# Two tiles of x loaded and normalized earlier, output-stage loads reordered, last output unit split: a hybrid decoder layer on eight cores

## The reference

```
h    = rmsnorm(x, norm_pre)                       # x (4, 4096, 2048)
proj = h @ w_in                                   # columns: xa ga u v gb q gc, 1024 each
ya = pool_mixer(xa) * silu(ga)                    # windows 2, 4, 8, 16, then 256x256 maps
yb = u * (tril(w_s) @ layernorm(v) + b) * silu(gb)   # chunks of 128 positions, 8 heads
yc = softmax(q k^T / 16) v_m * silu(gc)           # k, v_m = rmsnorm(mem) @ w_kv, 4 heads
y  = concat(rmsnorm(ya), rmsnorm(yb), rmsnorm(yc))   # 3072 columns
x  = x + rmsnorm(y @ w_out, norm_post)
```

## Time and profile before

| | us |
|---|---|
| median of three runs | 1258.14 |
| the profiled execution | 1258.87 |
| span of its slowest core (core 3) | 1257.2 |
| spans of cores 0, 1, 2 | 1256.9, 1253.4, 1251.3 |
| spans of cores 4, 5, 6, 7 | 1255.0, 1255.8, 1254.6, 1256.1 |
| PE busy on core 3 | 1220.3 (97%) |
| DVE, ACT, POOL busy | 488.0, 475.9, 216.0 |

### The profile page before, as it was taken

How to read it: one execution, slowest core, us unless ns; L and a number is a source line. 1 busy time by engine, 2 the same in 40 slices (tenths; PEclk the granted TensorE clock), 3 DMA queues, 4 the chain that set the end, 5 groups by cost and what they waited for, 6 DMA issues and landing times.

```text
span 1257.2 us, 17843 instructions; the slowest of 8 cores (1251.3 to 1257.2 us)
## 1 busy us (share of the span) xinstructions
PE 1220.3 (97%) x6224; PEld 582.0 (46%) x6224; DVE 488.0 (39%) x782; ACT 475.9 (38%) x892; POOL 216.0 (17%) x205
## 2 busy tenths in 40 slices
PE   6889999999999999999999999999989999999997
PEld 3345544444444455555554444444434444444443
DVE  4167624332232233444443233333222454343434
ACT  4377733422222232222225555555632232223222
POOL 1000001221211011111121111111222222222222
PEclk9999999999999999999999999999999999999999
DMA  9945322554234452645435541441975492533231
GB/s 210 245 152 173 69 81 68 105 90 83 50 67 81 83 93 45 107 88 91 97 63 98 86 82 34 81 88 34 178 212 138 129 307 75 178 133 118 93 109 68
DMA packets 50938, 137.83 MB, mean 110 GB/s; under 512 B 22785, under 2 KB 35201, under 8 KB 37137
## 3 DMA queue, kind: packets, MB, share of 16 engines
q0 software_dynamic: 7632, 50.86, 24.3%
q1 hardware_dynamic: 43218, 85.83, 21.3%
HBM read 153.39 MB, written 29.36 MB: 145 GB/s over the span
## 4 chain that ended last, share of the span: by engine, by line
PE 90%; DMA 3%; DVE 2%; ACT 2%; issue 1%; SPq 0%; DVEq 0%; POOLq 0%; POOL 0%; ACTq 0%
PE ps L279 89%; DMA mem_pages<-x 2%; DMA mem_pages<-y_scr 2%; PE ps L282 1%; ACT mem_pages L391 1%; DVE mem_pages L395 1%; DVE mem_pages L1155 0%; ACT mem_pages L1030 0%; SPq L291 0%; ACT L1030 0%; DVE stat L1025 0%; DVE mem_pages L1127 0%; DVE mem_pages L1035 0%; DVE mem_pages L545 0%; ACT stat L256 0%
## 5 line engine op out<-in xcount | busy, mean ns | idle before, releaser
L279 PE MATMUL ps<-mem_pages 128*128 128x512 bf16 (+2 forms) x5760 | 1195.7, 369 | 7.9 <-DMA mem_pages<-y_scr 4.0
L279 PEld LDWEIGHTS ps<-mem_pages 128*128 128x128 bf16 x5760 | 555.7, 98 | 630.5 <-issue 22.8
L713 POOL TENSOR_TENSOR mem_pages<-mem_pages 128x512 f32<-128x512 f32 x72 | 91.1, 1266 | 599.9 <-ACT mem_pages L706 597.3
L700 ACT ACTIVATE mem_pages<-mem_pages,small_c 128x512 bf16<-128x512 f32 x96 | 68.8, 716 | 275.4 <-DVE mem_pages L772 148.1
L1127 DVE SCALAR_TENSOR_TENSOR mem_pages<-ps,stat,mem_pages 128x512 f32<-128x512 f32 x128 | 96.0, 750 | 166.8 <-PE ps L279 144.4
L1135 POOL TENSOR_TENSOR mem_pages<-mem_pages 128x512 f32<-128x512 f32 x64 | 81.1, 1267 | 257.3 <-ACT jk L1132 257.3
L1132 ACT ACTIVATE jk<-mem_pages 128x512 bf16<-128x512 f32 x64 | 40.3, 629 | 224.0 <-DVE mem_pages L1127 224.0
L903 DVE TENSOR_TENSOR mem_pages<-mem_pages 128x526 f32<-128x526 f32 (+3 forms) x80 | 56.1, 701 | 100.8 <-ACT mem_pages L897 95.8
L762 DVE TENSOR_TENSOR mem_pages<-ps,mem_pages 128x512 f32<-128x512 f32 x32 | 22.1, 691 | 141.3 <-PE ps L279 141.3
L732 ACT ACTIVATE mem_pages<-ps 128x512 f32<-128x512 f32 x96 | 54.5, 590 | 22.8 <-PE ps L279 19.4
L748 DVE CAST mem_pages<-ps 128x512 bf16<-128x512 f32 (+1 forms) x24 | 14.4, 601 | 124.6 <-PE ps L279 121.4
(11 more groups left out here) (66 smaller groups left out, 422.9 us busy)
## 6 DMA issues: line engine op xcount, KB each, us to landing
mem_pages<-w_pages POOLq DMA_DIRECT2D x44, 1024.0 KB, 12.9
mem_pages<-x SPq DMA_DIRECT2D x32, 1024.0 KB, 7.8
out<-mem_pages SPq DMA_DIRECT2D x15, 1024.0 KB, 4.7
y_scr<-mem_pages SPq DMA_DIRECT2D x96, 128.0 KB, 1.9
mem_pages<-y_scr SPq DMA_DIRECT2D x12, 1024.0 KB, 14.6
mem_pages<-w_pages POOLq DMA_DIRECT2D x8, 512.0 KB, 19.7
mem_pages<-mem SPq DMA_DIRECT2D x2, 1024.0 KB, 6.2
mem_pages<-mem_norm SPq DMA_DIRECT2D x1, 1024.0 KB
```

The source lines that it names most:

```text
L279: return lambda e: e.matmul(out, lhsT=lhsT, rhs=rhs, start=start, stop=stop)
L700: P.op("act", lambda e: e.activation(out=yv, in_=tmp, func=AF.Copy, scale=gbr[:, c:c + 1]), reads=[tmp_b[i], gbr_b], writes=[ring_b[r]])
L713: P.op("pool", lambda e: e.tensor_tensor(out=accl_v if last else acc, in0=acc, in1=dst, op=ALU.add), reads=[dst_b, acc_b[tb]], writes=[acc ...
```

## The change

Five edits:

- The load of tile 4 waits for the first half of v page (0,0) instead of page (0,1); that of tile 5 for the second half of page (1,0) instead of the first half of page (1,1). Loads 6 and 7 are as they were.
- `x_a(4)` stands ahead of the half layer norms of tiles 0 to 3; two of these follow it at once, the other two follow the first half of tile 4's transposes.
- The matmuls of tile 3's second column half are spread between those of tiles 0 to 2, so that tile 0's last group comes one group earlier; and for tile 4 the products with page (1,0) go ahead of tile 5's transposes.
- In `out_q` the third weight load goes last; the gain is asked for from block 10, the branch results from block 12.
- The last output unit (tile 15, last 512 columns) is two units of 256 columns, with a sum of squares each in new columns of `stat`; the four final pieces stay.

```diff
-    x_load(4, [W2[0].wtok])
-    x_load(5, [W4[0].wtok])
+    x_load(4, [W1[0].wtok])
+    x_load(5, [W3[1].wtok])
...
             v_mm(tt, 0, 1, part)
-            if part == 1:
-                v_ln_half(tt, 0)
     x_a(4)
+    for tt in range(2):
+        v_ln_half(tt, 0)
...
     x_pe(4, (7, 7), (0,))
+    for tt in range(2, 4):
+        v_ln_half(tt, 0)
     v_mm(0, 1, 1, 0)
     v_mm(1, 1, 1, 0)
     x_pe(4, (7, 7), (1,))
     v_mm(2, 1, 1, 0)
-    v_mm(3, 1, 0, 0)
-    v_mm(3, 1, 0, 1)
     for tt in range(3):
+        v_mm(3, 1, tt // 2, tt % 2)
         v_mm(tt, 1, 1, 1)
         v_ln_half(tt, 1)
         v_ln_end(tt)
         if tt == 1:
             x_a(5)
-    v_mm(3, 1, 1, 0)
     v_mm(3, 1, 1, 1)
...
+        if tt == 4:
+            v_mm(tt, 1, 0)
         if tt + 1 < NTT:
             x_pe(tt + 1)
...
-        v_mm(tt, 1, 0)
+        if tt > 4:
+            v_mm(tt, 1, 0)
         v_mm(tt, 1, 1)
...
-    out_q = [(3, 0, lambda: wo_load(0)), (3, 0, lambda: wo_load(1)), (3, 0, lambda: wo_load(2)),
-             (3, 13, lambda: y_load(0)), (2, 0, gp_load)]
+    out_q = [(3, 0, lambda: wo_load(0)), (3, 0, lambda: wo_load(1)), (1, 10, gp_load), (3, 12, lambda: y_load(0)),
+             (3, 13, lambda: wo_load(2))]
...
-        for db in range(4):
-            wo_unit(tt, db)
-        wo_final(tt, last=tt == NTT - 1)
+        last = tt == NTT - 1
+        for db in range(3 if last else 4):
+            wo_unit(tt, db, so=ST_SL + db if last else None)
+        if last:
+            wo_unit(tt, 3, 0, 256, ST_SL + 3)
+            wo_unit(tt, 3, 256, 256, ST_SL + 4)
+        wo_final(tt, last)
```

More of the change, by code:

```diff
@@ L249, in build_program @@
     ST_LH0, ST_LH1 = 352, 360
+    ST_SL = 368
     ST_EPS = 383
@@ L547, in v_ln_end @@
              reads=[bank[b], bank[b + 1], s1], writes=[vn_b[tt]])
-    W2, W3, W4 = wbuf(("v", 0, 1)), wbuf(("v", 1, 0)), wbuf(("v", 1, 1))
+    W1, W3, W4 = wbuf(("v", 0, 0)), wbuf(("v", 1, 0)), wbuf(("v", 1, 1))
     x_a(0)
@@ L1101, in take_orow @@
         p = dyn()
-        orow[tt] = (p, [nbuf("or%d_%d" % (tt, db), p) for db in range(4)], nbuf("orr%d" % tt, p))
+        orow[tt] = (p, [nbuf("or%d_%d" % (tt, db), p) for db in range(5)], nbuf("orr%d" % tt, p))
     def load_xres(tt):
@@ L1108, in load_xres, with wo_unit @@
         xres[tt] = (p, b)
-    def wo_unit(tt, db):
+    def wo_unit(tt, db, lo=0, n=512, so=None):
         tb = tt // 4
+        so = ST_SO + tt * 4 + db if so is None else so
         p, obs, _ = orow[tt]
-        ov = page_f(p)[:, db * 512:(db + 1) * 512]
+        ob = obs[db + (1 if lo else 0)]
+        c0 = db * 512 + lo
+        ov = page_f(p)[:, c0:c0 + n]
         bks = []
@@ L1118, in wo_unit @@
             Wo = w8(("wo", db, br))
-            fns = [mm(psb(b), yv[:, q, (tt % 4) * 128:(tt % 4 + 1) * 128], Wo[:, q, :], q == 0, q == 7)
+            fns = [mm(psb(b, 0, n), yv[:, q, (tt % 4) * 128:(tt % 4 + 1) * 128], Wo[:, q, lo:lo + n], q == 0, q == 7)
                    for q in range(8)]
@@ L1123, in wo_unit @@
         rc = ST_RBR + tt
-        P.op("act", lambda e: e.activation(out=ov, in_=psb(bks[0]), func=AF.Identity, scale=sc(rc)),
-             reads=[bank[bks[0]], rbr_b[tb]], writes=[obs[db]])
+        P.op("act", lambda e: e.activation(out=ov, in_=psb(bks[0], 0, n), func=AF.Identity, scale=sc(rc)),
+             reads=[bank[bks[0]], rbr_b[tb]], writes=[ob])
         for br in (1, 2):
             P.op("dve", lambda e, br=br: e.scalar_tensor_tensor(
-                out=ov, in0=psb(bks[br]), scalar=sc(rc + br * 16), in1=ov, op0=ALU.mult, op1=ALU.add),
-                reads=[bank[bks[br]], rbr_b[tb], obs[db]], writes=[obs[db]])
+                out=ov, in0=psb(bks[br], 0, n), scalar=sc(rc + br * 16), in1=ov, op0=ALU.mult, op1=ALU.add),
+                reads=[bank[bks[br]], rbr_b[tb], ob], writes=[ob])
         bfree(*bks)
[L1131 to L1134, removed]
+        P.op("act", lambda e: e.activation(out=jk_v[:, 0:n], in_=ov, func=AF.Square, scale=D ** -0.5,
+                                           accum_out=sc(so)),
+             reads=[ob], writes=[jk_b, so_b[tt]])
+        gv = page_f(gp["p"])[:, c0:c0 + n]
         P.op("pool", lambda e: e.tensor_tensor(out=ov, in0=ov, in1=gv, op=ALU.mult),
-             reads=[obs[db], gp["b"]], writes=[obs[db]])
+             reads=[ob, gp["b"]], writes=[ob])
     so_b = [Buf("so%d" % t) for t in range(NTT)]
@@ L1142, in wo_final @@
         stf = Buf("stf")
-        c0 = ST_SO + tt * 4
-        P.op("dve", lambda e: e.reduce_sum(out=sc(ST_FO + tt), in_=stat[:, c0:c0 + 4], axis=AX.X),
+        c0, cn = (ST_SL, 5) if last else (ST_SO + tt * 4, 4)
+        P.op("dve", lambda e: e.reduce_sum(out=sc(ST_FO + tt), in_=stat[:, c0:c0 + cn], axis=AX.X),
              reads=[so_b[tt]], writes=[stf])
@@ L1147, in wo_final @@
         xp, xb = xres[tt]
-        n = 4 if last else 1
-        w = 2048 // n
         rows = out_d[tt * 128:(tt + 1) * 128, :]
[L1151 to L1154, removed]
+        pieces = [(q, 1, obs[q:q + 1] if q < 3 else obs[3:]) for q in range(4)] if last else [(0, 4, obs)]
+        for q, n, ob in pieces:
+            o = page_f(p)[:, q * 512:(q + n) * 512]
+            xv = page_f(xp)[:, q * 512:(q + n) * 512]
             P.op("dve", lambda e, o=o, xv=xv: e.scalar_tensor_tensor(out=o, in0=o, scalar=sc(ST_FR + tt), in1=xv,
@@ L1157, in wo_final @@
                  reads=[stf, xb] + ob, writes=ob)
-            dma_sp(rows[:, q * w:(q + 1) * w], o, reads=ob, sem="d_o%d_%d" % (tt % 4, q))
+            dma_sp(rows[:, q * 512:(q + n) * 512], o, reads=ob, sem="d_o%d_%d" % (tt % 4, q))
         drop(p, xp)
```

## The result

The changed kernel took 1245.40 and 1246.18 us, the kernel before 1257.67 to 1259.98 (median 1258.62): a ratio of 0.9897 with a 95% interval of 0.9873 to 0.9921, about 13.0 us less (9.9 to 16.0), against 13.2 forecast.

A forecast was written before the change was run, and what follows sets the result against it. PE, busy 97% of the span, was taken as the bound, so gains lay only in its waits, slow stretches and tail. 7.0 + 5.6 + 0.6 = 13.2 us off gave 1244.9 us, range 1243.0 to 1248.0, chance 75%.

The forecast's parts named there:

- The start: First v products: tile 4's 4.49 wait and 1.67 slow stretch go, tile 0's last group comes 0.86 earlier; 7.0 us gained.
- The weights and tile 5: Loads at the start: earlier tiles delay the last two v half pages by up to 1.5; loss taken 0, bounds 0 to 2.
- a matmul group waiting for v weights: At the start: a sign that would show the prediction wrong, beside tile 4 landing after 40 or hand-over loads issued together.
- equal halves: Loads at the start: x and weights sharing engines evenly, each tile costing the weights 5.8 instead of 2.2 us.
- The product of tile 4: Start: putting it ahead of tile 5's transposes only moves where PE waits; value 0, at most a few tenths either way.
- The hand-over: First output unit: branch results asked for 15 us earlier remove 4.0 of waits and 1.7 of slow pace; 5.6 taken.
- core 5 waited less than core 3: Hand-over: cores that waited less gain less; core 5, 2.19 at the last wait, no slow pace, ends level with core 3.
- The tail: Last output unit in two halves: matmuls +0.10, addition -0.3, Square -0.2, closing operation -0.17; 0.6 us gained, bounds +0.1 and -1.0.
- exclusive lock: Tail, DVE's first closing operation beside POOL's multiplication: by the skill's rule the loss would be 0.38, not 0.17.
- The weights as a wait: Second rival, at the start: late v weights start ACT's chain at 58.7, the start gives nothing, 1251.9 us; chance 12%.
- That the hand-over fails: Third rival: a page is missing at block 12, transfers meet as before, nothing of the 5.6, 1250.5 us; chance 7%.
- Tile 4 was not served last: Fourth rival, at the start: tile 4, asked for among the weights, lands at 61.5; kernel slower at 1268.3 us; chance 4%.

The follow-up runs named there:

- Experiments 6: Changed kernel with the loads of tiles 4 and 5 waiting for the same weights as before, new order of work kept: 1246.08 and 1246.50 us.
- experiment 7: Kernel before with only the two earlier loads of tiles 4 and 5, order of work as before: 1259.15 us, ratio 1.0004.
- Experiment 10: Changed kernel with the first gate page's weights asked for only when tile 7 has landed: 1245.81 us, ratio 0.9895 to the kernel before.
- Experiment 9: Changed kernel with tile 4's product with page (1,0) behind tile 5's transposes again: 1245.76 us, ratio 0.9894 to the kernel before.
- experiment 3: Kernel before, branch results still asked for at block 13, third output weight set moved to block 14, gain behind it: 1264.76 us, ratio 1.0043.
- experiment 4: Kernel before, third output weights after block 14, and the y stores' ring page given back last in block 15: 1253.17 us, ratio 0.9954.
- experiment 2: Kernel before with only the new order of out_q loads at the hand-over: 1253.39 us, ratio 0.9952.
- experiment 1: Changed kernel with out_q and the last output unit as before, so only the start's edits: 1251.2 us, ratio 0.9935 to the kernel before.

## Why the prediction was right, step by step

**The start, 7.0: right.** On core 4 tile 4's Square stood at 33.99 (33.9 forecast), ACT's chain at 51.16 (51.05), the granted clock was full, and the chain's end came 7.2 earlier where nothing else waited (39.75 against a median of 46.9). Alone it gave 8.2 (5.7 to 10.6). Experiments 6 and 7 correct the weight that the steps have in it: I told the earlier load first, but `x_a(4)`'s place in ACT's order carries the gain, and the load is worth up to 1.8 of PE's wait on a core, and less than can be told in the time.

**The weights and tile 5, taken at 0: too low for some cores.** Three cores waited 0.83, 0.60 and 0.54 for tile 5 itself and a fourth 1.09 for the last half page of v weights:

```profile
50.28 5.34 PE L280 MATMUL ps<-mem_pages 128*128 128x512 bf16 x23 [1.09 <-DMA mem_pages<-w_pages]
```

Their chain ended 0.65 to 1.25 later. The prediction's bound was 0 to 2, so it held, but one of its own signs of being wrong, a matmul group waiting for v weights, did appear on that core. The sentence that failed is that tile 5 "was not what the chain waited for": true in the trace of before, but the chain now wanted the tile 7.0 earlier. The tile was asked for earlier too, and landed no earlier: on core 4 it was issued at 44.00 and took 12.6 in the kernel before, and was issued at 41.75 and took 15.3 now, so that it is there at 56.6 and 57.05. The first two fences are of before, the third of the changed kernel:

```profile
44.00 0.33 SPq L291 DMA_DIRECT2D mem_pages<-x  x1
```

```profile
mem_pages<-x SPq DMA_DIRECT2D x1, 1024.0 KB, 12.6
```

```profile
41.75 0.33 SPq L292 DMA_DIRECT2D mem_pages<-x  x1
```

So on the three cores that waited for it (0, 4 and 6) this part of the edit bought nothing: the tile is there 25.4 to 25.9 us behind the start of the 64 matmuls, and was 25.3 to 25.8 on the same cores before. (Core 3, which did not wait, had it 2.3 earlier.) Experiment 10 shows that the tile met the gate page: 9.0 without it. The Trainium skill (DMA: Bandwidth & Descriptors, Queues, rings and completion order) has each DMA engine go round-robin between the queues that have work. The direction agrees with 15.3 against 9.0. The prediction's reading of it as equal halves, by which ACT's chain would have started at 58.7, does not: it started at 51.16.

**The product of tile 4, taken at 0: right.** Experiment 9 moves the waits and nothing else.

**The hand-over, 5.6: right.** Alone it gave 6.0 (4.3 to 7.7), with no wait on any core, and by the cause that was given, transfers that met (experiments 3 and 4). The prediction's aside that core 5 waited less than core 3 is a misreading: its three waits are 0.56, 1.71 and 2.19, 4.46 together against 4.01, and it gained less only because it had no slow pace. What I didn't see is the inherited wait on the ring page. It stands in the changed kernel as well, and an estimate shows how close it is: PE stopped 18.5 us after the start of the first unit in experiment 3, which on core 4 of the changed kernel would be 921.4, and ACT's wait ends there at 918.24, so it is harmless by some 2 us.

**The tail, 0.6: right up to the last stores, and hidden behind them on the slowest core.** Up to the first closing operation it took 2.28 us instead of 2.76, and the four closing operations 2.74 instead of 2.91:

```profile
1250.91 2.91 DVE L1155 SCALAR_TENSOR_TENSOR mem_pages<-mem_pages,stat 128x512 f32<-128x512 f32 x4 [0.17 <-DVE stat L258]
```

That row is core 3 of before, from which the earlier trace rows shows the first of the four. Its difference to 2.74 is the 0.17 of the prediction. The Trainium skill (SBUF — State Buffer, SBUF: two separate sides) has an exclusive lock between two such operations. By POOL's recorded end, and POOL's times in a profile are rough, that would have given 0.38; the trace says 0.17. DVE's 256 columns took 0.48 (0.45 taken), ACT's 0.42 (0.43). The step that failed is the one that carried this gain to the end of the slowest core at full size: from the first closing operation to the end of the span core 4 needed 6.61, core 3 of before 6.29, so 8.9 remained instead of 8.4. The prediction had no term for the last stores. That the gain itself is there is seen on cores 6 and 7 of the changed kernel, with 7.7 and 7.6 from the last matmul to the end, against 8.2 to 8.3 on cores 0, 1, 6 and 7 of before: 0.6, on cores whose neighbour's span is 1.2 us or more away. On core 4 the neighbour's is 0.4 away.

**The rivals.** The weights as a wait came to 1.1 at most, not 7. That the hand-over fails is refuted by experiment 2. Tile 4 was not served last: it landed in 11.3 to 13.3 us. The prediction's range of 1243.0 to 1248.0 was narrower than its bounds, from which it said that it came: 1, 4.0 and -0.1 add up to 4.9 at the low end, which would be 1253.2.

**The sum.** Apart the three parts give 8.2 + 6.0 + 0.9 = 15.1, together 13.0. The intervals overlap, and each part alone is seen on the slowest core of its own kernel, so the difference is not one that the runs settle. That 13.0 fell so close to 13.2 is partly luck: tile 5 and the last stores each took some tenths that the sum did not have, and the interval of the measurement, 9.9 to 16.0, is far wider than the distance.

## What to carry to other kernels

When a tile is late, look first at what stands ahead of it on the engine that prepares it: here the same load came 7 us earlier for nothing until its Square was moved up. Two sets of transfers that are both early enough can still be late because they run together; pull them apart, and then check from whom each buffer inherits its waits. A chain that has become the bound of a stretch is shown by shortening it, as the pairing of the norms' ends did.

## What the runs showed of the hardware

- The last megabyte's stores, from the first closing operation to the end of the span, go with what the neighbouring core does (0 and 1, 2 and 3, ...). In all thirteen profiles of this case, 104 cores, they took 6.4 to 7.6 us on all 26 cores whose neighbour's span was within 0.5 us, and 5.3 to 5.7 on 30 of the 38 whose neighbour's was 1.2 or more away; between these, 5.5 to 7.1. The eight exceptions (5.8 to 6.6) are six times core 2 or 3, and cores 0 and 1 of experiment 7. That neighbours storing at once slow each other is argued from this, not shown: no experiment kept them apart. If it holds, cores that are levelled give back about 1.4 us at the end (an estimate, 6.9 against 5.5 by the medians of the two groups).
- The last stores of y (128 KB each), which land 2.1 and 2.6 us after their issue in the kernel before (core 3), took 11.5 and 17.9 in experiment 3 and 12.3 and 18.5 in experiment 4 (core 4), beside pages of output weights.
- How long PE waited at the hand-over does not tell whether it runs slowly behind it. In the kernel before the waits of core 3 (4.0 us in three pieces) and core 6 (3.4 in two) were followed by 9.62 us for 36 matmuls, with a granted clock of 0.50 from 918 to 920 us on core 3. Those of core 5 (4.5 in three) and core 7 (5.1 in three) were followed by 7.93, with a granted clock of 1.00 on core 5. In experiment 1 it was 2.9 us on core 7 that brought the slow pace, and 5.1 on core 5 that did not. What sets them apart is open.
